# A two-block transformer on one core: first feature group of each layer in token-major form, halves staggered, fill matmuls in waits

## The reference

```python
def rmsnorm(x, g):
    return x * lax.rsqrt(mean(x * x) + 1e-6) * g
# first block, i = 0 (fox_attention) and i = 1 (short_conv)
    m = mixer(rmsnorm(x, g[0]))
    x = x + rmsnorm(m, g[1])
    f = square(relu(rmsnorm(x, g[2]) @ w_mlp_up)) @ w_mlp_down      # 1024 -> 4096 -> 1024
    x = x + rmsnorm(f, g[3])
    gate = sigmoid(rmsnorm(x, g[4]) @ w_ple_gate)
    x = x + rmsnorm((p @ w_ple_proj) * gate, g[5])
# second block, layer 0 (rwkv7_time_mix), layer 1 (diff_attention, with shared_kv before it)
    x = x + mix(rms_norm(x, g_mix))
    x = x + (silu(h @ w_gate) * (h @ w_up)) @ w_down                # h = rms_norm(x, g_ffn), 1024 -> 2816 -> 1024
```

## Time and profile before

| | us |
|---|---|
| median of 3 runs | 1687.5 |
| lowest, highest run | 1686.6, 1690.42 |
| span of the profiled execution (first to last instruction) | 1691.7 |

### The profile page before, as it was taken

How to read it: one execution, slowest core, us unless ns; L and a number is a source line. 1 busy time by engine, 2 the same in 40 slices (tenths; PEclk the granted TensorE clock), 3 DMA queues, 4 the chain that set the end, 5 groups by cost and what they waited for, 6 DMA issues and landing times.

```text
span 1691.7 us, 24256 instructions
## 1 busy us (share of the span) xinstructions
PE 1567.7 (93%) x9802; PEld 1373.8 (81%) x9802; DVE 979.4 (58%) x1251; ACT 724.6 (43%) x931; POOL 136.1 (8%) x112
## 2 busy tenths in 40 slices
PE   7999999977998999868989999989999799899998
PEld 7966899866988999657668888879999686689997
DVE  4554565555566655549776565655655475456554
ACT  4443554445445544435632222244444363345443
POOL 2000111100000111000212212000000020000000
PEclk8999999988999999988988999989999896699999
DMA  7612465543654555524530000026565352045553
GB/s 252 187 61 76 144 213 186 191 145 123 189 162 156 198 187 187 163 100 124 170 112 26 1 2 1 1 86 208 169 210 174 127 189 64 13 162 189 186 163 124
DMA packets 81823, 229.15 MB, mean 135 GB/s; under 512 B 11729, under 2 KB 17553, under 8 KB 81713
## 3 DMA queue, kind: packets, MB, share of 16 engines
q1 hardware_dynamic: 81584, 227.54, 41.7%
q0 software_dynamic: 128, 0.07, 0.0%
HBM read 226.46 MB, written 1.05 MB: 134 GB/s over the span
## 4 chain that ended last, share of the span: by engine, by line
PE 87%; DVE 8%; ACT 3%; issue 1%; POOL 1%; DMA 1%; SPq 0%; DVEq 0%; ACTq 0%; POOLq 0%
PE PS L404 50%; PE PS L407 33%; PE PS L419 4%; ACT SH L376 1%; DVE X L619 1%; DVE SL L382 1%; DVE LG L1341 1%; DVE XL L518 1%; ACT JK L597 0%; DVE XN L596 0%; DVE XI L1061 0%; POOL SM L609 0%; DVE SL L379 0%; DVE XT L1349 0%; DVE XT L1350 0%
## 5 line engine op out<-in xcount | busy, mean ns | idle before, releaser
L382 DVE SCALAR_TENSOR_TENSOR SL<-ST,SM,SH 128x1024 fp32r<-128x1024 f32 (+1 forms) x256 | 317.0, 1258 | 242.3 <-ACT SH L376 233.9
L404 PE MATMUL PS<-XH,SH 128*128 128x256 f32 x1568 | 443.7, 283 | 8.3 <-DVE XL L518 8.3
L407 PE MATMUL PS<-XH,SL 128*128 128x256 f32 x1568 | 444.5, 283 | 0.0
L404 PE MATMUL PS<-XL,SH 128*128 128x256 f32 x1568 | 443.3, 283 | 0.0
L376 ACT ACTIVATE SH<-ST,SM 128x1024 fp32r<-128x1024 f32 (+1 forms) x256 | 281.1, 1121 | 289.4 <-PE PS L407 271.8
L379 DVE TENSOR_TENSOR SL<-ST,SH 128x1024 fp32r<-128x1024 f32 (+1 forms) x167 | 213.5, 1295 | 171.4 <-ACT SH L376 154.1
L404 PEld LDWEIGHTS PS<-XH,SH 128*128 128x128 f32 x1568 | 301.3, 192 | 10.6 <-ACT XH L517 5.7
L404 PEld LDWEIGHTS PS<-XL,SH 128*128 128x128 f32 x1568 | 298.0, 190 | 0.6
L407 PEld LDWEIGHTS PS<-XH,SL 128*128 128x128 f32 x1568 | 298.1, 190 | 0.0
L376 ACT ACTIVATE SH<-ST 128x1024 fp32r<-128x1024 f32 (+1 forms) x167 | 172.1, 1047 | 193.4 <-PE PS L407 184.4
L404 PE MATMUL PS<-SH,XH 128*128 128x512 f32 (+1 forms) x432 | 178.1, 412 | 29.9 <-ACT XH L517 8.4
(11 more groups left out here) (306 smaller groups left out, 1744.3 us busy)
## 6 DMA issues: line engine op xcount, KB each, us to landing
ST<-in_ffn_w_gu SPq DMA_DIRECT2D x80, 512.0 KB, 4.7
ST<-in_w_mlp_up SPq DMA_DIRECT2D x64, 512.0 KB, 4.7
ST<-in_w_mlp_down SPq DMA_DIRECT2D x64, 512.0 KB, 4.3
ST<-in_ffn_w_down SPq DMA_DIRECT2D x44, 512.0 KB, 4.4
ST<-in_w_attn_in SPq DMA_DIRECT2D x24, 512.0 KB, 3.7
ST<-in_w_conv_in SPq DMA_DIRECT2D x24, 512.0 KB, 3.6
ST<-in_w_ple_gate SPq DMA_DIRECT2D x16, 512.0 KB, 3.6
ST<-in_kv_w SPq DMA_DIRECT2D x16, 512.0 KB, 4.4
```

The source lines that it names most:

```text
L382: b = ve.do(lambda e: e.scalar_tensor_tensor(l[p0:p1, 0:cols], t[p0:p1, 0:cols], sc, h[p0:p1, 0:cols].bitcast(F32), ALU.mult, ALU.subtract ...
L404: pe.go(lambda e: e.matmul(o, l, r, start=start, stop=stop, skip_group_check=skip))
L407: return pe.do(lambda e: e.matmul(o, l, r, start=start, stop=stop, skip_group_check=skip))
```

## The change

1. **Buffers.** 6 split and 4 stage buffers instead of 5 and 5, so splits run 5 units ahead; 2 parameter buffers instead of 3.
2. **Staggered halves.** `enter` replaces `raw_t` at the eight entries. `kind_a` with `end=True` keeps 4 units by half (EDGE) instead of 3. Then: `chain(0)` (norm and addition of half 0), fill matmuls, half 0's transposes, a fill, `ahead(2, po)` (two splits whose low part is made by GpSimd, the gain applied beforehand by ScalarE in place), `chain(1)`, then a `kind_a` whose first 4 units run for half 0, with half 1's transposes put in after the third, then for half 1. In ple the two embedding units follow `chain(0)`.
3. **First group token-major.** That `kind_a` computes the first group (mlp: 1024 features; conv: the gate; ffn: 512 + 512), which was `kind_b`. The result, after its activation, is turned with 16 transposes (ffn: 8) and split between the units of the next group. In ple and kv the product was `kind_a` already.
4. **Start.** The raw x is transposed and normed afterwards; the forget logits come after the queries, with 24 matmuls of 256 columns.
5. **Fills.** `keep_busy(n, b)` issues n matmuls of constants, 512 columns in float32, into a free bank: 2+1 in mlp, ffn and kv, 0 in ple, 1+1 in conv, 8 and 2 in the mix of layer 2, 8+1 and 4+1 at the two output projections of block 2, 1 before and 2 in each of the first three steps of the differential attention.
6. **Moved.** The six small DMAs for lambda and the head norms, and the VectorE and ScalarE work on them, go from before the kv entry to the first attention. Adding and norming is issued per half everywhere. The last FFN groups are 256, 512 instead of 512, 256.

```diff
-NSPLIT, NSTAGE, NPAR = 5, 5, 3
...
     ai, ci = A["w_attn_in"][0], A["w_conv_in"][0]
-    u(ai[:, 3072:3088].rearrange("(k p) n -> p k n", p=128), 128, gain="f")
     for c in range(3):
         for k in range(8):
             u(rows(ai, k, c * 1024, c * 1024 + 1024), gain=k)
+        if c == 0:
+            u(ai[:, 3072:3088].rearrange("(k p) n -> p k n", p=128), 128, gain="f")
     for k in range(8):
         u(rows(A["w_attn_out"][0], k, 0, 1024))
...
-    FG = [512] * 5 + [256]
+    FG = [512] * 4 + [256, 512]
...
-    def unit_split():
+    def unit_split(lo=ve):
...
+        if g is not None and lo is po:
+            ready = ac.do(lambda e, g=g: e.activation(t[p0:p1, 0:cols], t[p0:p1, 0:cols], ACT.Copy, scale=GT[:, g:g + 1]), ready, t_gt)
+            g = None
         sc = 1.0 if g is None else GT[:, g:g + 1]
...
         if g is None:
-            b = ve.do(lambda e: e.tensor_tensor(l[p0:p1, 0:cols], t[p0:p1, 0:cols], h[p0:p1, 0:cols].bitcast(F32), ALU.subtract),
+            b = lo.do(lambda e: e.tensor_tensor(l[p0:p1, 0:cols], t[p0:p1, 0:cols], h[p0:p1, 0:cols].bitcast(F32), ALU.subtract),
...
-    def kind_a(xs, kbs, banks, first=True, last=True, xt=None, end=False):
+    def kind_a(xs, kbs, banks, first=True, last=True, xt=None, end=False, mid=None, look=LOOK):
...
-        if end:
-            cut = sum(len(g) for g in groups) - 3
-            groups = [g for g in groups if g[-1] < kbs[0] + cut] + [kbs[cut:]]
+        head = EDGE if xt is not None and len(kbs) >= EDGE else 0
+        tail = EDGE if end else 0
+        groups = ([kbs[0:head]] if head else []) + [[k] for k in kbs[head:len(kbs) - tail]] + ([kbs[len(kbs) - tail:]] if tail else [])
         assert sum(len(g) for g in groups) == len(kbs)
         for g in groups:
-            us = take_group(len(g))
+            lead = head and g is groups[0]
+            us = take_group(len(g), len(g) - 1 if lead else look)
             for m in range(2):
-                if xt is not None and g is groups[0]:
-                    pe.wait(xt[m])
-                for k, (i, h, l) in zip(g, us):
+                for j, k in enumerate(g):
+                    i, h, l = us[j]
                     pe.wait(split_tok[i])
+                    if lead and j == 0:
+                        pe.wait(xt[m])
                     for n in range(2):
                         ls = [x[:, k, m * 128:(m + 1) * 128] for x in xs]
                         rs = [x[:, n * 512:(n + 1) * 512] for x in (h, l)]
+                        if first and k == kbs[0]:
+                            pe.wait(bfree[banks[2 * m + n]])
                         tok[m] = mm3(bank(banks[2 * m + n]), ls, rs, first and k == kbs[0], last and k == kbs[-1])
-            for i, _, _ in us:
-                pe_done[i] = tok[1]
+                    if m:
+                        pe_done[i] = tok[m]
+                    elif lead and mid is not None and j == len(g) - 2:
+                        mid()
         return tok
...
+    def ahead(n=1, lo=ve):
+        for _ in range(n):
+            if n_split[0] < len(units) and (n_split[0] < NSPLIT or n_split[0] - NSPLIT in pe_done):
+                unit_split(lo)
+    def keep_busy(n, b, c=C_LV, w=512):
+        pe.wait(bfree[b])
+        for _ in range(n):
+            mm(bank(b, 0, w), CC[:, 0:128], CC[:, c:c + w], True, True)
...
+    def enter(chain, tb, banks, fill, between=None, **kw):
+        r = [None, None]
+        chain(0)
+        if between is not None:
+            between()
+        keep_busy(fill[0], tb[0][0])
+        r[0] = raw_half(0, tb[0])
+        keep_busy(fill[1], banks[0])
+        ahead(2, po)
+        chain(1)
+        def second():
+            r[1] = raw_half(1, tb[1])
+        return kind_a(XS[0], range(8), banks, xt=r, mid=second, end=True, **kw)
...
                     softmax(h)
+            if diff and j < 3:
+                keep_busy(2, 7)
...
         tv.append(res)
-    norm_t(None, 0, 0)
+    xparts[0], xparts[1] = [t_x[0]], [t_x[1]]
+    xh = []
+    for m in range(2):
+        xh.append(raw_half(m, (2 * m, 2 * m + 1)))
+        ahead()
+    rt = raw_rstd()
...
+    pe.wait(xh)
+    wait_banks([4, 5, 6, 7])
+    kind_b(XS[0], range(4), (4, 5, 6, 7), last=False)
+    rest_of_constants()
+    tsb = row_scale(rt, 0)
+    sbb = SBT[:, :].unsqueeze(1).to_broadcast([128, 4, S])
+    def evac_s(dst, banks, tok, scale, *toks):
+        r = []
+        for z in range(2):
+            ps = PS[:, banks[2 * z] * 512:banks[2 * z] * 512 + 1024].rearrange("p (b t) -> p b t", b=4)
+            r.append(ve.do(lambda e, ps=ps, z=z: e.scalar_tensor_tensor(dst[:, 4 * z:4 * z + 4, :], ps, scale, sbb, ALU.mult, ALU.mult), tok, tsb, *toks))
+            bfree[banks[2 * z]] = bfree[banks[2 * z + 1]] = r[z]
...
+    t = kind_b(XS[0], range(4, 8), (4, 5, 6, 7), first=False)
+    tq = evac_s(QT, (4, 5, 6, 7), t, 0.125, rt)
...
+    wait_banks([1])
+    for k in range(8):
+        t = mm3(bank(1, 0, 256, 0, 16), [x[:, k * 16:k * 16 + 16] for x in (h, l)], [x[:, k, :] for x in XS[0]], k == 0, k == 7)
+    pe_done[i] = t
+    a = ac.do(lambda e: e.activation(FT[:, :], bank(1, 0, 256, 0, 16), ACT.Copy), t)
+    wait_banks([0, 2, 3, 4, 5])
+    kind_b(XS[0], range(2), (2, 3, 4, 5), last=False)
+    pe.wait(a)
     for m in range(2):
-        for k in range(8):
-            t = mm3(bank(m, 0, 16), [x[:, k, m * 128:m * 128 + 128] for x in XS[0]],
-                    [x[:, k * 16:k * 16 + 16] for x in (h, l)], k == 0, k == 7)
-    pe_done[i] = t
-    rest_of_constants()
+        t = mm_t(bank(0, m * 16, m * 16 + 16), FT[:, m * 128:m * 128 + 128], CC[0:16, 0:16], True, True)
...
+    a = ve.do(lambda e: e.tensor_tensor(LM[:, 5:6], LM[:, 3:4], LM[:, 2:3], ALU.subtract), a)
+    a = ve.do(lambda e: e.tensor_scalar(NLAM, LM[:, 5:6], LAM_INIT, None, ALU.subtract), a)
...
+    def mlp(layer, chain, P, fill, tail_free):
+        Q = 4 - P
+        acc, grp = (P, P + 1, P + 2, P + 3), (Q, Q + 1, Q + 2, Q + 3)
+        ob = (Q + 2, Q + 3, P, P + 1)
+        t0 = enter(chain, ((Q, Q + 1), (P + 2, P + 3)), ob, fill)
...
+        R = HR[0]
+        RN_, HN = ar(f"RN{layer}", 6, [128, 2, D]), ar(f"HN{layer}", 8, [128, 2, D])
+        h0 = []
+        for m in range(2):
+            ps = PS[:, ob[2 * m] * 512:ob[2 * m] * 512 + 1024]
+            a = ac.do(lambda e, ps=ps, m=m: e.activation(RN_[:, m, :], ps, ACT.Relu), t0[m], hr_free[0])
+            b = ve.do(lambda e, ps=ps, m=m: e.scalar_tensor_tensor(HN[:, m, :], ps, 0.0, RN_[:, m, :], ALU.max, ALU.mult), a)
+            bfree[ob[2 * m]] = bfree[ob[2 * m + 1]] = b
+            h0.append(b)
...
-        for g in range(4):
-            bs = (0, 1, 2, 3) if g else (4, 5, 6, 7)
-            wait_banks(bs)
-            t = kind_b(XS[0], range(8), bs)
+        wait_banks(grp)
...
+        hx[0].append(transpose_split(HN[:, 1, :], h0[1], 1, (P, P + 1), HX[0], None, hx_free[0]))
+        hr_free[0] = list(hx[0])
+        for g in range(1, 4):
+            if g > 1:
+                wait_banks(grp)
+            t = kind_b(XS[0], range(3 if g == 1 else 0, 8), grp, first=g > 1)
...
+    def ple(i, before, P):
...
+        def embed():
+            wait_banks(eb)
+            pe.wait(xs_tok)
+            emb.append(kind_a(xs, range(2), eb, look=0))
+        tg = enter(mlp_chain, ((P, P + 1), (P + 2, P + 3)), acc, (0, 0), embed)
...
+    tc = enter(ple_chain, ((0, 1), (2, 3)), (4, 5, 6, 7), (1, 1))
...
+        cn.append(ac.do(lambda e, m=m, ps=ps: e.activation(CN[:, m, :], ps, ACT.Copy, scale=S2[:, m:m + 1]), tc[m], pw, hx_free))
+        bfree[4 + 2 * m] = bfree[5 + 2 * m] = cn[m]
...
+        cs = slice(m * 128, m * 128 + 128)
+        return ac.do(lambda e: e.activation(CG[:, :, cs], ps, ACT.Copy), t, hr_free[0])
     wait_banks([0, 1, 2, 3])
-    t = kind_b(XS[0], range(8), (0, 1, 2, 3))
+    kind_b(XS[0], range(2), (0, 1, 2, 3), last=False)
+    cg = [transpose_split(CN[:, 0, :], cn[0], 0, (4, 5), None, to_cg)]
+    kind_b(XS[0], range(2, 3), (0, 1, 2, 3), first=False, last=False)
+    cg.append(transpose_split(CN[:, 1, :], cn[1], 1, (6, 7), None, to_cg))
...
     m2 = mix(2, 0)
+    keep_busy(8, 4)
...
     i, h, l = take()
+    keep_busy(2, 3)
...
+    keep_busy(8, 4)
     res = [transpose_split(Ra[:, m, :], ([y_res[0]], [y_res[1]]), m, (2 * m, 2 * m + 1), XS[0], None, scan_done) for m in range(2)]
     q = res[1]
+    keep_busy(1, 4)
...
+    def ffn(chain):
+        t0 = enter(chain, ((0, 1), (6, 7)), (2, 3, 4, 5), (2, 1))
...
         for g, n in enumerate(FG):
-            bs = (0, 1, 2, 3) if g else (4, 5, 6, 7)
-            wait_banks(bs)
             if g == 0:
-                pe.wait(xt)
-                kind_b(XS[0], range(3), bs, nblk=2 * n // 128, last=False)
-                tsb.append(row_scale(rt, 0))
-                t = kind_b(XS[0], range(3, 8), bs, nblk=2 * n // 128, first=False)
...
+    t = enter(chain0, ((0, 1), (2, 3)), (4, 5, 6, 7), (2, 1))
...
-    wait_banks([4, 5, 6, 7])
```

(4 more changed lines are left out.)

364 lines of the change are left out of this document (193 added, 171 removed).

## The result

| | us |
|---|---|
| median of 4 runs of the change | 1728.2 (1727.3 to 1730.1) |
| ratio to the kernel before | 1.0239, 95% interval 1.0219 to 1.0259 |
| predicted | 1645 (1624 to 1670), 0.975 of before |
| span of the profiled execution, before and after | 1691.7, 1725.7 |

The change is slower by 2.4%, and the prediction was wrong in sign. The kernel before gives two groups of times, 1686 to 1694 and 1714 to 1727 us; the ratio goes by the first, and what parts them is the subject of half of the experiments.

What follows compares the result with a forecast made beforehand. The prediction took TensorE, 87% of the chain, as the bound, losing time in waits and at its lower clock. Terms -6 - 18 - 9 - 6.5 - 3 = -42.5 took 1691.7 to 1649 us, the median to 1645 (1624 to 1670).

Steps and rivals of the forecast that it cites:

- ple: The two ple entries: four units done at 30.4 us against 30.5 and 30.2 before, so 0, twice.
- The first attention: First attention stage: no term for a loss, 0; its row was read as 36 us at clock 1.00.
- (b): Differential attention: fills bring the full clock, 57 us become about 38, -18; nothing gained if the clock stays at 0.50.
- a fill into the first wait and two into each step: Differential attention: six fills at 0.43 us, 2.6 in sum, in steps whose matmuls use only 64 rows, for the full clock.
- was entered at full clock, this one at 0.50: Argument comparing the two attentions: the first entered at full clock, the differential at 0.50 after two waits of 1.3 us.
- the clock stays low: Rival: the differential attention's clock stays low despite the fills, 1668 us; chance 0.18.
- (a): The eight layer entries with staggered halves: -6 in sum, between -43 and +25; each ffn entry +1.7.
- with 8 transposes 18.0: Ffn entry: four units done at 16.9 us, 18.0 with the result's 8 transposes, against 16.3 before: +1.7, twice.
- (c): The start: raw x transposed at once, products at about 11 us instead of 24; -9, between -5 and -12.
- five units split in advance: Kv entry, -8.6: VectorE's 6.05 us small-DMA wait moves to the first attention, under 13.9 us of cover.
- pays for itself and no more: Mlp 0 entry: stagger gives 19.9 against 20.1 us; the result's 16 transposes then add 2.1, making +1.9.
- The rival of the slower side: Two `ahead` splits at each entry, GpSimd subtractions at 3.0 us, delay half 1 and lower the clock; about 1692 us, chance 0.05.

Runs made afterwards that it cites:

- e3: Kernel before with 4 fill matmuls ahead of the first scores of the first attention; 10 runs: 1690.0, 1695.4, eight at 1718.6 to 1728.7 us.
- e5: Kernel before with one fill ahead of the transposes of heads 0 and 1 of the first attention; 12 runs, 1688.7 to 1694.9 us.
- e13: Kernel before with the change's buffer numbers alone (6 split, 4 stage, 2 parameter); 1695.0 us, 11 runs.
- e14: Kernel before with the 6 fills of the differential attention alone; 1715.5 us, 10 runs at 1684.4 to 1726.6.
- e12: The change with 2 fills ahead of the first scores of the first attention; 7 runs, six at 1693.6 to 1700.8, one at 1731.5 us.
- e4: The change with the row scale's two VectorE operations in each FFN put ahead of the first units of group 1; 1713.0 us.
- e15: e10 with the row scale's VectorE part ahead of the first units at the start and in both FFNs; 1668.9 us, ratio 0.9889.
- e10: The change with e9's old first groups, e5's two fills, e2's late lambda work, e6's values' banks, no entry or differential-attention fills; 1673.8 us, ratio 0.9912.
- e8: The change without the fills of the entries, the other fills kept; 1715.4 us, 4 runs.
- e9: The change with the first group of both MLPs and both FFNs made as before, without stagger or fills there; 1705.6 us, 4 runs.
- e2: The change with VectorE's wait for the lambda DMAs and its work on them put behind the keys' evacuation; 1722.8 us, 10 runs.
- e6: Change with two first-attention fills, one fill per differential-attention head pair, late lambda work, early row-scale VectorE part, values' product on banks keys leave free; 1672.6 us.
- e7: The change with half 1's norm and addition ahead of the two `ahead` splits in each entry; 1730.2 us, 4 runs.

## Why the prediction was wrong

The stages of the table other than start, first attention, FFNs and differential attention sum to -17.8 in the trace (+2.0 - 2.4 - 2.8 + 3.5 - 2.2 - 4.7 - 3.8 - 7.4), and the prediction's terms for them to -17.8 as well (+1.9 - 4.6 + 2.0 - 6.5 - 2 - 8.6). In part that is luck: ple gave 2.3 each where I had 0, and the mixer's -3.8 is no gain at all, as the old mixer took 358.2 to 359.0 in e3, e5, e13 and e14, less than the 360.6 of the change. The other 76 us, from -42.4 to +34.0, are four steps.

1. **The first attention, +29.1 against 0.** No term and no rival had it. I read its row, "36 us at 1.00 with TensorE 99% busy", as proof that this stage holds the clock, when it was one draw of two: by its times, the same kernel ran this stage at the low clock in 47 of 89 runs. The three runs of before that were known then all lay in the lower group. The evidence that this stage was unsure was in the prediction: 45 us of nearly the same matmuls at 0.50 with TensorE never idle. I asked what could raise the clock there and not what could lower it here. That the loss is this clock, and that the old code has the fall too, is shown by e3, e5 and e12; why the change fell in every run stays open.
2. **(b), the differential attention and its output, +0.4 against -19.** What failed is that "a fill into the first wait and two into each step" would raise the clock for good: each pair of fills raises it, and it falls when they end. Three stretches of after, behind the first pair, around the second and behind the last:

```profile
1439.00:1442.00 3.00, 3.00 (x12) 1.89 (x13) 0.62 (x2) 0.79 (x4) 0.00 (x0) 0.96 0.00 0
1443.00:1446.00 3.00, 3.00 (x7) 1.07 (x5) 1.53 (x6) 0.83 (x4) 0.00 (x0) 0.63 0.00 0
1457.00:1460.00 3.00, 3.00 (x8) 1.66 (x7) 1.18 (x4) 1.08 (x5) 0.00 (x0) 0.50 0.00 0
```

   The argument for it was a misreading: that the first attention "was entered at full clock, this one at 0.50". The stretch of the earlier trace rows begins at 1412, behind the fall. The kernel before enters this stage at the full clock too, with its first scores at 1409.24, and drops 1.5 us later:

```profile
1406.00:1409.00 3.00, 1.97 (x16) 1.73 (x16) 1.17 (x1) 1.84 (x3) 0.00 (x0) 1.00 0.56 171
1409.00:1410.50 1.50, 1.26 (x5) 0.78 (x5) 0.00 (x0) 1.10 (x2) 0.00 (x0) 1.00 0.00 0
1410.50:1413.00 2.50, 2.50 (x7) 1.47 (x6) 0.62 (x2) 0.92 (x4) 0.00 (x0) 0.54 0.02 7
```

   So a high clock at the entry was not what this stage lacked. My rival "the clock stays low" was the nearest, with a chance of 0.18. The fill's price was half of the true one. The Trainium skill (TensorE: Matmul & The Clock Gate, Part 1, the HAM clock gate) ties the full rate to how busy the engine has been; in the first attention of the change the profile has TensorE busy for 100% of 90 us, and it had the full rate for a quarter of that, so the row goes on contradicting the rule for this mix of small matmuls.
3. **(a), the FFNs, +20.2 against +3.4.** The entry came out as worked (half 0, the low parts, half 1, each about 1 us late). What failed is where I stopped: "with 8 transposes 18.0" counted the transposes and not the row scale behind them, whose VectorE part had been moved behind two copies and up to six splits. The rule to name what is queued behind a moved step was followed for ScalarE and GpSimd and not for VectorE. e4 gives 6.0 and 6.8 us of it back in the two FFNs, e15 against e10 2.6 and 4.1, e8 1.6 and 2.2. e13 shows that the buffer numbers alone make 1.7 us of the wait; in e9, without the new first groups, it is 3.7.
4. **(c), the start, +2.1 against -9.** The products started at 12.3, as the prediction had it within 1.3. Lost were 2.7 at the row scale and 6.4 at the keys' evacuation, and behind that wait 4.4 us ran at the low clock. In the kv entry I had written that VectorE's wait for the small DMAs would be covered by five units split in advance. It was not: TensorE's own next step needed VectorE for the evacuation. e2 and e6 give 3.3 and 6.0 back.

That an entry's stagger "pays for itself and no more" was right for the MLPs: e7 shows the order of the change to be the better one, and e9 that undoing the new first group gives back 2.0 and 3.7. The fills of the entries were to keep the clock at 0.43 each; they cost 0.86 each, and by e8 the kernel is better without them. The rival of the slower side, GpSimd's subtractions at 3.0 us, did not occur: the 16 took 2382 ns each.

```profile
L384 POOL TENSOR_TENSOR SL<-ST,SH 128x1024 fp32r<-128x1024 f32 x16 | 37.8, 2382 | 294.0 <-ACT SH L381 294.0
```

## What to carry to other kernels

A clock of 1.00 in a stretch of light matmuls was here the result of one run, not a property of the stage. Where a similar stage runs at 0.50 in the same trace, try a dense matmul or two behind the last heavy unit before anything else is tuned, and run the kernel before often enough to see whether it has one group of times or two. Fills are path work at their full price (two records in float32) and belong only where a trace shows the fall. When a step moves, write down for every in-order queue what now stands ahead of the small operations that TensorE waits for; a wait hoisted into a covered stretch is covered only if nothing behind it on that queue is needed there.

## What was not expected of the hardware

- TensorE, busy without a gap, held 1.2 GHz for 68 us in the first attention (107 to 175) and for 65 us in e3, while the same 277 matmul records ran at 2.4 GHz throughout in the traces of the kernel before and of e12. The times of the kernel before fall into two groups with medians 28.8 us apart and nothing between 1694.3 and 1714.5 in 89 runs.
- Two fills of 0.9 us each, in the two steps behind the last dense unit, removed the upper group (12 of 12 runs). Ahead of the first scores, two fills brought six of seven runs of the change to the high clock, one fill none of four, and four fills in the kernel before only two of ten.
- A float32 matmul of 512 columns appears as two records and takes 0.86 us at the high clock, where one with rounded operands takes 0.23.
